# One more Strassen block in three of the four down-projection pairs of a hybrid decoder layer

## The chip, the cores and the metric

The kernel runs on one core of one Trainium2 chip. The metric is the device time in microseconds (us) of one execution, as the median of several runs. Engine names are those of the profile: PE is TensorE, DVE is VectorE, ACT is ScalarE, POOL is GpSimd, SP is SyncE; PEld is PE's loading of its stationary operand.

## What is computed

One layer of a hybrid decoder trunk on 256 tokens of width 2048: an RG-LRU branch and an attention branch, merged; a cross attention; and a SwiGLU feed-forward of inner width 5632, whose last product, the down projection, is what the change touches.

```python
def swiglu(h, w_gate, w_up, w_down):
    return (jax.nn.silu(h @ w_gate) * (h @ w_up)) @ w_down
...
    h = rmsnorm(x, norm_ffn_g[l])
    x = x + swiglu(h, w_ffn_gate[l], w_ffn_up[l], w_ffn_down[l])
return rmsnorm(x, norm_final_g)
```

## The kernel before

Every large product is done in split single precision. A weight tile `w_raw` (256 rows of the weight, as two tiles of 128, by 512 columns, 512 KB) is loaded by SP's queue. ACT rounds it to `w_hi` (L838), DVE takes the rest `w_lo` (L1228), and PE adds three matmuls for each product (L473 to L475): hi by hi, hi by lo, lo by hi. A **chunk** is one such weight tile in one of R = 4 slots. PE consumes chunks in order. ACT writes `w_hi` of chunk m when PE has finished chunk m-4, DVE follows with `w_lo`, and PE waits for that before chunk m. On ACT and DVE the function `splits` runs a stage's other work of chunk c first and then the weight step of chunk c+4, so everything on these engines stands in one fixed order.

Most stages are **pairs**: two groups of 512 output columns (two PSUM buffers, `group0` and `group1`) are made together over the same activations. A plan lists the steps, each for a k pair kp (256 values of k). `O5` makes two ordinary chunks, O5a for the first group and O5b for the second, of 12 matmuls each. `W4` makes a **Strassen block**: four chunks A, B, C, D of 6, 3, 6 and 6 matmuls, 21 in place of 24. A and B are loaded; C and D are sums of weight tiles, which DVE makes in `weight_sums` (L1243, L1244, L1246) just ahead of `w_lo` of A. A block also needs sums of activations, made once for each k pair (L1367 to L1370 on DVE, L870 on ACT, L1376 on DVE) and kept. `T6+7+8+9` makes four k pairs for the first group and then the same four for the second.

Four of the seven Strassen products of a block go to the extra PSUM tensors `side0` and `side1`. After the last D chunk of a pair, `fold_rest` and `first_fold` put them into the SBUF tile `fold` (ACT L876, DVE L1385, L1386, L1388, L1389) at chunks last_sum+1 and last_sum+2. At last_sum+3 and last_sum+4 DVE adds `fold` to the residual `x_res` (L1710, or L1734 in the last pair), once for each half of the tokens. At the last two chunks of a pair (counts -2 and -1) `add_group` (L1581) adds the two PSUM groups to `x_res`, and this hands the group's buffer to the next pair: PE may not start the next pair's first chunk of a group before it.

The feed-forward runs in two parts, a (six gate/up pairs, then two down pairs over 12 k pairs) and b (five gate/up pairs, then two down pairs over 10). The gate/up pair j makes four tiles of the inner activations, which are transposed and split during the next pair (`inner_split`, `inner_rest`); where `F_SUMS` names the k pair 2(j-1), its activation sums are made there too. Two steps of the final norm lie in the last down pair, ("b", 2): `squares` (ACT L885) at chunks 1 and 3, and `gained` (DVE L1719) at chunks 6 and 8. The last four chunks are made token half by token half, so that the first half's tail runs beside the second's products.

Of the kernel before, what the change touches and what calls it, by code (L numbers as in the profile page):

```python
# [56 lines left out]
for _j in range(1, KG):  # L57
# [8 lines left out]
RNN_PLANS = {0: "T0+1 O3 W2 O5 W4 O6 O7".split(), 2: "O0 O1 W2 O3 O5 W4 O6 O7".split()}  # L66
KEY_PLAN = "O0 O1 W3 O2 O4 W5 O6 O7".split()
FIRST_UP_PLAN = "O0 O1 O2 W3 O4 W5 O6 O7".split()
DOWN_PLAN = {("a", 0): "O0 O1 O3 W2 O5 O7 W4 O8 W6 O9 O10 O11".split(),
             ("a", 2): "O0 O1 W2 O3 O5 W4 O7 W6 O9 W8 O10 O11".split(),  # L70
             ("b", 0): "O0 O1 O3 O5 W2 O6 W4 O7 O8 O9".split(),
             ("b", 2): "O0 O1 W2 O3 W4 O5 T6+7+8+9".split()}
R_SUMS = [int(_step[1:]) for _step in RNN_PLANS[0] if _step[0] == "W"]
K_SUMS = [int(_step[1:]) for _step in KEY_PLAN if _step[0] == "W"]
X_SUMS = [int(_step[1:]) for _step in UP_PLAN if _step[0] == "W"]
F_SUMS = {_part: sorted({int(_step[1:]) for (_of, _j), _plan in DOWN_PLAN.items() if _of == _part for _step in _plan if _step[0] == "W"})
          for _part in ("a", "b")}
# [27 lines left out]
for _part, _groups in (("a", FA), ("b", FB)):  # L105
    for _j in range(_groups):
        PLACED.append((("gate_" + _part, _j), ("up_" + _part, _j), FIRST_UP_PLAN if (_part, _j) == ("a", 0) else UP_PLAN))
    for _j in range(0, KG, 2):
        PLACED.append((("down_" + _part, _j), ("down_" + _part, _j + 1), DOWN_PLAN[_part, _j]))
_n = _g = 0  # L110
# [1693 lines left out]
```

How the kernel before makes its waits and increments, by code:

```python
        def wait_product(engine, end):  # L303
            s, used = slot_of(end - 1)
            engine.wait_ge(w_used[s], START + used + 1)
# [1 line left out]
        def wait_taken(engine, g):  # L308
            p, before = buf_of(g)
            engine.wait_ge(taken[p], START + before + 1)
# [3 lines left out]
        @block.sync  # L315
# [1 line left out]
            def load(n, w, row, col):  # L317
                s, _ = raw_of(n)
                if LOAD_OF[n] >= R:
                    earlier, used = slot_of(LOADED[LOAD_OF[n] - R])
                    sync.wait_ge(w_ready[earlier], START + used + 1)
                sync.dma_start(raw[:, s], w[row:row + CK * P, col:col + GW].rearrange("(k p) n -> p k n", p=P)).then_inc(raw_full[s], 16)
# [20 lines left out]
                sync.dma_start(raw[:, 0, k], w_in[k * P:(k + 1) * P, IN_COLS["g_rnn"]:IN_COLS["g_rnn"] + GW]).then_inc(signal, 16)  # L344
            for n, (name, c) in enumerate(OPENING):
                if name == "g_rnn" and c > 0:
                    x_pair(c)
                if n > 0:
                    load(n, w_in, c * CK * P, IN_COLS[name])
            for j in range(KG):
                if j > 0:
                    in_group("g_rnn", j)
                if j >= 2:
                    sync.wait_ge(sem("lru_z"), j - 1)
                for a, gate in enumerate(("lru_w_a", "lru_w_i")):
                    sync.dma_start(lw[j % 2][:, a], dram[gate][j * NB:(j + 1) * NB, :, :].rearrange("n k m -> k n m"))\
                        .then_inc(sem(f"lw_full{j % 2}"), 16)
```

## Time and profile before

| | |
|---|---|
| median of 3 runs | 1751.98 us (1751.96 to 1752.61) |
| profiled execution, first to last instruction | 1750.0 us |
| PE busy | 1738.3 us (99%) |
| DVE busy | 1287.1 us (74%) |
| ACT busy | 974.8 us (56%) |
| mean DMA rate | 193 GB/s |

The profiled execution is known by its span alone; it lies 1.98 us below the median of the timed runs. Matmuls overlap, so PE reads as busy nearly always: what one costs is the distance from its start to the next one's start. Times in the trace's rows are microseconds from the start of the span.

### The profile page before, as it was taken

To read this page: it belongs to the slowest core of one execution; us is meant where nothing else is said; L and a number is where in the kernel's file an instruction comes from. 1 tells how busy PE (TensorE), PEld (TensorE's weight loads), DVE (VectorE), ACT (ScalarE), POOL (GpSimd) and SP (SyncE) were. 2 spreads that over 40 slices of the span, in tenths; PEclk is the share of its full clock that TensorE was granted. 3 is DMA by queue.
4 is the path that set the end of the run, shared out by engine and by line. 5 is a ranking of instruction groups with operands and counts; after the bars stand their busy time and mean duration, and the time that the engine had idled before them with its cause. 6 is when DMAs were issued, how large, how long until landed. Compare 5 with 4: busy or idle time off the path is not lost.

```text
span 1750.0 us, 20314 instructions
## 1 busy us (share of the span) xinstructions
PE 1738.3 (99%) x7923; PEld 1442.6 (82%) x7923; DVE 1287.1 (74%) x1404; ACT 974.8 (56%) x1211; POOL 28.8 (2%) x54
## 2 busy tenths in 40 slices
PE   9999999999999999999999999999999999999998
PEld 7888888888888888888888888888888888888886
DVE  7677687887575757555565579888888788888787
ACT  6767668554555555544455465555555545555554
POOL 1100000000000000000000000000000000000000
PEclk9999999999999999999999999999999999999999
DMA  8565665666565655556755455566666565666664
GB/s 292 172 204 166 196 201 162 204 203 204 157 212 166 216 168 189 174 187 206 250 186 187 140 174 185 191 197 196 194 204 213 183 206 192 193 193 195 216 201 158
DMA packets 176047, 338.22 MB, mean 193 GB/s; under 512 B 10704, under 2 KB 15312, under 8 KB 175696
## 3 DMA queue, kind: packets, MB, share of 16 engines
q1 hardware_dynamic: 173376, 327.98, 59.5%
q0 software_dynamic: 1296, 5.24, 0.9%
q10 hardware_dynamic: 1280, 3.71, 0.5%
q8 instruction: 62, 1.02, 0.2%
q14 instruction: 33, 0.27, 0.1%
HBM read 334.80 MB, written 2.10 MB: 193 GB/s over the span
## 4 chain that ended last, share of the span: by engine, by line
PE 97%; DVE 1%; ACT 0%; issue 0%; DMA 0%; ACTq 0%; POOLq 0%; POOL 0%; DVEq 0%
PE group L473 29%; PE group L475 29%; PE group L474 29%; PE side L473 2%; PE side L474 2%; PE side L475 2%; PE side L536 2%; DVE w_lo L1228 0%; PE side L670 0%; PE side L654 0%; DMA x_T_in<-in_x_T 0%; PE side L608 0%; PE side L607 0%; PE side L606 0%; DVE x_res L1581 0%
## 5 line engine op out<-in xcount | busy, mean ns | idle before, releaser
L838 ACT ACTIVATE w_hi<-w_raw 128x1024 fp32r<-128x1024 f32 x612 | 622.4, 1028 | 538.5 <-PE group L475 437.2
L1228 DVE TENSOR_TENSOR w_lo<-w_raw,w_hi 128x1024 fp32r<-128x1024 f32 x612 | 711.8, 1184 | 281.4 <-ACT w_hi L838 275.0
L473 PE MATMUL group<-w_hi,x_hi 128*128 128x512 f32 x1460 | 573.3, 393 | 0.8 <-DVE w_lo L1296 0.6
L475 PE MATMUL group<-w_hi,x_lo 128*128 128x512 f32 x1460 | 568.8, 390 | 0.0
L474 PE MATMUL group<-w_lo,x_hi 128*128 128x512 f32 x1460 | 568.2, 389 | 0.0
L473 PEld LDWEIGHTS group<-w_hi,x_hi 128*128 128x128 f32 x1460 | 274.1, 188 | 59.1 <-DVE w_lo L1228 1.9
L475 PEld LDWEIGHTS group<-w_hi,x_lo 128*128 128x128 f32 x1460 | 274.0, 188 | 57.6
L474 PEld LDWEIGHTS group<-w_lo,x_hi 128*128 128x128 f32 x1460 | 274.2, 188 | 55.6
L838 ACT ACTIVATE w_hi<-w_sums 128x1024 fp32r<-128x1024 f32 x86 | 91.3, 1061 | 150.2 <-PE group L475 104.6
L1228 DVE TENSOR_TENSOR w_lo<-w_sums,w_hi 128x1024 fp32r<-128x1024 f32 x86 | 104.8, 1222 | 52.5 <-ACT w_hi L838 52.3
L473 PE MATMUL group<-w_hi,v_hi 128*128 128x512 f32 x296 | 115.9, 392 | 0.0
L475 PE MATMUL group<-w_hi,v_lo 128*128 128x512 f32 x296 | 115.2, 389 | 0.0
L474 PE MATMUL group<-w_lo,v_hi 128*128 128x512 f32 x296 | 115.1, 389 | 0.0
L473 PE MATMUL group<-w_hi,inner_hi 128*128 128x512 f32 x286 | 111.6, 390 | 0.0
L475 PE MATMUL group<-w_hi,inner_lo 128*128 128x512 f32 x286 | 111.3, 389 | 0.0
L474 PE MATMUL group<-w_lo,inner_hi 128*128 128x512 f32 x286 | 111.3, 389 | 0.0
L1243 DVE TENSOR_TENSOR w_sums<-w_raw 128x1024 f32<-128x1024 f32 x43 | 52.5, 1221 | 43.6 <-issue 21.3
L475 PEld LDWEIGHTS group<-w_hi,v_lo 128*128 128x128 f32 x296 | 55.6, 188 | 11.6
L473 PEld LDWEIGHTS group<-w_hi,v_hi 128*128 128x128 f32 x296 | 55.6, 188 | 11.3
L474 PEld LDWEIGHTS group<-w_lo,v_hi 128*128 128x128 f32 x296 | 55.6, 188 | 11.3
L475 PEld LDWEIGHTS group<-w_hi,inner_lo 128*128 128x128 f32 x286 | 53.7, 188 | 11.3
L473 PEld LDWEIGHTS group<-w_hi,inner_hi 128*128 128x128 f32 x286 | 53.7, 188 | 11.3 <-DVE x_res L1581 0.3
(304 smaller groups left out, 1714.4 us busy)
## 6 DMA issues: line engine op xcount, KB each, us to landing
w_raw<-in_w_in SPq DMA_DIRECT2D x223, 512.0 KB, 4.2
w_raw<-in_w_ffn_gate SPq DMA_DIRECT2D x88, 512.0 KB, 3.9
w_raw<-in_w_ffn_up SPq DMA_DIRECT2D x88, 512.0 KB, 4.6
w_raw<-in_w_ffn_down SPq DMA_DIRECT2D x88, 512.0 KB, 4.8
w_raw<-in_w_rnn_proj SPq DMA_DIRECT2D x32, 512.0 KB, 4.8
w_raw<-in_w_attn_proj SPq DMA_DIRECT2D x32, 512.0 KB, 4.2
w_raw<-in_w_mix_out SPq DMA_DIRECT2D x32, 512.0 KB, 3.7
w_raw<-in_w_xkv SPq DMA_DIRECT2D x16, 512.0 KB, 3.8
```

Source lines behind the costliest of these rows:

```text
L473: nc.tensor.matmul(out, h, whi[:, s, k, :], start=start, stop=False)
L474: nc.tensor.matmul(out, h, wlo[:, s, k, :], start=False, stop=False)
L475: return nc.tensor.matmul(out, l, whi[:, s, k, :], start=False, stop=stop)
L536: last = nc.tensor.transpose(dst[:, k, tt * P:(tt + 1) * P], src[:, tt, k * P:(k + 1) * P], ident)
L838: nc.scalar.activation(whi[:, s, ks], src[:, ks], ACT.Copy).then_inc(hi_ready[s], 1)
L1228: V_.tensor_tensor(wlo[:, s, ks], src[:, ks], whi[:, s, ks].bitcast(F32), ALU.subtract).then_inc(w_ready[s], 1)
L1243: then(V_.tensor_tensor(w_sums[:, :, 0, :], tiles[:, a:a + 4:3, :], tiles[:, a + 2:a + 3, :].to_broadcast([P, 2, GW]), ALU.add))
```

## The change

Only the table of plans changes. In ("a", 0) four blocks (kp 2, 4, 6, 8) replace three (2, 4, 6); in ("b", 0) three (2, 4, 6) replace two (2, 4); in ("b", 2) three (2, 4, 6) replace two (2, 4). ("a", 2) stays.

```diff
-DOWN_PLAN = {("a", 0): "O0 O1 O3 W2 O5 O7 W4 O8 W6 O9 O10 O11".split(),
+DOWN_PLAN = {("a", 0): "O0 O1 O3 W2 O5 W4 O7 W6 O9 W8 O10 O11".split(),
              ("a", 2): "O0 O1 W2 O3 O5 W4 O7 W6 O9 W8 O10 O11".split(),
-             ("b", 0): "O0 O1 O3 O5 W2 O6 W4 O7 O8 O9".split(),
-             ("b", 2): "O0 O1 W2 O3 W4 O5 T6+7+8+9".split()}
+             ("b", 0): "O0 O1 O3 W2 O5 W4 O7 W6 O8 O9".split(),
+             ("b", 2): "O0 W2 O1 W4 O3 W6 T5+7+8+9".split()}
```

`F_SUMS` is worked out from this table. Part a keeps 2, 4, 6, 8. Part b goes from 2, 4 to 2, 4, 6, so the activation sums of kp 6 are made anew, in the gate/up pair ("gate_b", 4).

The block nearest to the end of a pair moves later, and with it the fold. DVE at the end of ("a", 0), a piece of the difference:

```order
 L1228 TENSOR_TENSOR w_lo<-w_raw,w_hi 128x1024
 L1710 TENSOR_TENSOR x_res<-x_res,fold 128x1024
+L1581 TENSOR_TENSOR x_res<-x_res,group 128x2x512
 L1228 TENSOR_TENSOR w_lo<-w_raw,w_hi 128x1024
 L1710 TENSOR_TENSOR x_res<-x_res,fold 128x1024
-L1228 TENSOR_TENSOR w_lo<-w_raw,w_hi 128x1024
-L1581 TENSOR_TENSOR x_res<-x_res,group 128x2x512
-L1228 TENSOR_TENSOR w_lo<-w_raw,w_hi 128x1024
 L1581 TENSOR_TENSOR x_res<-x_res,group 128x2x512
 L1228 TENSOR_TENSOR w_lo<-w_raw,w_hi 128x1024
```

The two additions of the fold (L1710) and the two additions of the groups (L1581) stood in four different chunks and stand in two now.

DVE at the end of ("b", 0) and the start of ("b", 2), before:

```order
929 L1710 TENSOR_TENSOR x_res<-x_res,fold 128x1024
930 L1228 TENSOR_TENSOR w_lo<-w_raw,w_hi 128x1024
931 L1710 TENSOR_TENSOR x_res<-x_res,fold 128x1024
932 L1228 TENSOR_TENSOR w_lo<-w_raw,w_hi 128x1024
933 L1581 TENSOR_TENSOR x_res<-x_res,group 128x2x512
934 L1228 TENSOR_TENSOR w_lo<-w_raw,w_hi 128x1024
935 L1581 TENSOR_TENSOR x_res<-x_res,group 128x2x512
936 L1228 TENSOR_TENSOR w_lo<-w_raw,w_hi 128x1024
937 L1243 TENSOR_TENSOR w_sums<-w_raw 128x2x512
```

and in the changed kernel:

```order
946 L1710 TENSOR_TENSOR x_res<-x_res,fold 128x1024
947 L1581 TENSOR_TENSOR x_res<-x_res,group 128x2x512
948 L1243 TENSOR_TENSOR w_sums<-w_raw 128x2x512
949 L1244 TENSOR_TENSOR w_sums<-w_sums,w_raw 128x512
950 L1246 TENSOR_TENSOR w_sums<-w_sums,w_raw 128x512
951 L1228 TENSOR_TENSOR w_lo<-w_raw,w_hi 128x1024
952 L1710 TENSOR_TENSOR x_res<-x_res,fold 128x1024
953 L1581 TENSOR_TENSOR x_res<-x_res,group 128x2x512
954 L1228 TENSOR_TENSOR w_lo<-w_raw,w_hi 128x512
```

The next pair's first block has moved from its chunk 4 to its chunk 2, so its weight sums (L1243, L1244, L1246) have come to stand between the two L1581, where they stood behind both.

DVE in the middle of ("b", 2), around the two `gained` steps (L1719), before:

```order
944 L1719 TENSOR_TENSOR x_res<-x_res,gain_final 128x2x512
945 L1243 TENSOR_TENSOR w_sums<-w_raw 128x2x512
946 L1244 TENSOR_TENSOR w_sums<-w_sums,w_raw 128x512
947 L1246 TENSOR_TENSOR w_sums<-w_sums,w_raw 128x512
948 L1228 TENSOR_TENSOR w_lo<-w_raw,w_hi 128x1024
949 L1228 TENSOR_TENSOR w_lo<-w_raw,w_hi 128x512
950 L1719 TENSOR_TENSOR x_res<-x_res,gain_final 128x2x512
951 L1228 TENSOR_TENSOR w_lo<-w_sums,w_hi 128x1024 x2
```

and in the changed kernel:

```order
957 L1243 TENSOR_TENSOR w_sums<-w_raw 128x2x512
958 L1244 TENSOR_TENSOR w_sums<-w_sums,w_raw 128x512
959 L1246 TENSOR_TENSOR w_sums<-w_sums,w_raw 128x512
960 L1228 TENSOR_TENSOR w_lo<-w_raw,w_hi 128x1024
961 L1228 TENSOR_TENSOR w_lo<-w_raw,w_hi 128x512
962 L1719 TENSOR_TENSOR x_res<-x_res,gain_final 128x2x512
963 L1228 TENSOR_TENSOR w_lo<-w_sums,w_hi 128x1024 x2
964 L1719 TENSOR_TENSOR x_res<-x_res,gain_final 128x2x512
```

The two `gained` steps stood on both sides of the second block's weight sums; now they stand on both sides of its `w_lo` of C and D. SP's queue issues the same 217 rows in the same order in both kernels.

## Rows read from the trace of the kernel before

**Rows 1.** The page: the span, and each engine's busy time.

```profile
span 1750.0 us, 20314 instructions
...
PE 1738.3 (99%) x7923; PEld 1442.6 (82%) x7923; DVE 1287.1 (74%) x1404; ACT 974.8 (56%) x1211; POOL 28.8 (2%) x54
```

**Rows 2.** PE's waits from 20 us on: total us, times, longest us.

```profile
PE side L473 <- DVE w_lo L1228: 0.5, 1, 0.5
PE group L473 <- DVE x_res L1581: 0.2, 1, 0.2
```

**Rows 3.** Timeline, PE, the last products: start, duration, engine, line, out<-in.

```profile
1735.61 0.39 PE L473 MATMUL group<-w_hi,inner_hi 128*128 128x512 f32 x1
...
1742.19 0.39 PE L475 MATMUL group<-w_hi,inner_lo 128*128 128x512 f32 x1
```

**Rows 4.** Timeline, DVE, from the end of ("a", 2) into ("gate_b", 0).

```profile
1417.19 1.22 DVE L1581 TENSOR_TENSOR x_res<-x_res,group 128x1024 f32<-128x1024 f32 x1
1418.33 1.22 DVE L1228 TENSOR_TENSOR w_lo<-w_raw,w_hi 128x1024 fp32r<-128x1024 f32 x1
1419.46 1.22 DVE L1710 TENSOR_TENSOR x_res<-x_res,fold 128x1024 f32<-128x1024 f32 x1
1420.71 1.22 DVE L1581 TENSOR_TENSOR x_res<-x_res,group 128x1024 f32<-128x1024 f32 x1
...
1422.99 1.22 DVE L1243 TENSOR_TENSOR w_sums<-w_raw 128x1024 f32<-128x1024 f32 x1
...
1425.68 1.82 DVE L1228 TENSOR_TENSOR w_lo<-w_raw,w_hi 128x1024 fp32r<-128x1024 f32 x2
```

**Rows 5.** Timeline, PE, the same place; in brackets idle time and its releaser.

```profile
1421.37 0.39 PE L475 MATMUL group<-w_hi,x_lo 128*128 128x512 f32 x1
1421.99 0.50 PE L473 MATMUL group<-w_hi,x_hi 128*128 128x512 f32 x1 [0.23 <-DVE x_res L1581]
1422.33 0.40 PE L474 MATMUL group<-w_lo,x_hi 128*128 128x512 f32 x1
```

**Rows 6.** Timeline, ("gate_b", 3): activation sums on DVE, and PE just behind.

```profile
1562.32 0.28 DVE L1367 TENSOR_TENSOR inner_sums<-inner_T_in 128x128 f32<-128x128 f32 x1
```

```profile
1564.35 0.39 PE L475 MATMUL side<-w_hi,x_sums_lo 128*128 128x512 f32 x1
1564.64 0.50 PE L473 MATMUL group<-w_hi,x_hi 128*128 128x512 f32 x1
```

**Rows 7.** Timeline, ("b", 2): DVE, then PE, then ACT.

```profile
1709.91 1.22 DVE L1719 TENSOR_TENSOR x_res<-x_res,gain_final 128x1024 f32<-128x1024 f32 x1
1711.05 2.35 DVE L1228 TENSOR_TENSOR w_lo<-w_sums,w_hi 128x1024 fp32r<-128x1024 f32 x2
1713.32 4.63 DVE L1228 TENSOR_TENSOR w_lo<-w_raw,w_hi 128x1024 fp32r<-128x1024 f32 x4
...
1712.32 0.50 PE L473 MATMUL side<-w_hi,inner_sums_hi 128*128 128x512 f32 x1 [0.54 <-DVE w_lo L1228]
...
1697.85 0.62 ACT L885 ACTIVATE junk<-x_res 128x512 f32<-128x512 f32 x1
...
1699.61 1.06 ACT L838 ACTIVATE w_hi<-w_sums 128x1024 fp32r<-128x1024 f32 x1 [0.43 <-PE group L475]
```

**Rows 8.** Stretches behind the last matmul: us, busy of PE, ..., PEclk, DMA.

```profile
1742.60:1747.20 4.60, 0.00 (x0) 0.00 (x0) 2.21 (x6) 2.06 (x5) 0.55 (x1) 1.00 0.69 260
1747.40:1750.00 2.60, 0.00 (x0) 0.00 (x0) 0.00 (x0) 0.00 (x0) 0.00 (x0) 0.50 0.59 232
```

**Rows 9.** Weight tiles: an issue, the median time to landing, ACT's longest wait here.

```profile
1410.61 0.37 SPq L323 DMA_DIRECT2D w_raw<-in_w_ffn_up  x1
...
w_raw<-in_w_ffn_down SPq DMA_DIRECT2D x88, 512.0 KB, 4.8
...
1680.06 1.06 ACT L838 ACTIVATE w_hi<-w_raw 128x1024 fp32r<-128x1024 f32 x1 [3.90 <-DMA w_raw<-in_w_ffn_down]
```

**Rows 10.** Timeline, DVE, the second token half of the output's tail.

```profile
1742.61 0.75 DVE L1748 TENSOR_TENSOR x_res<-x_res,group 128x256 f32<-128x256 f32 x2 [0.81 <-PE group L475]
```

## The prediction, made before the changed kernel ran

> **What bounds the kernel now.** I read the page first, then PE's waits, then the timeline of DVE, ACT and PE at the seams between the down pairs. PE is busy for 99% of the span [rows 1] and behind the opening waits for anyone only twice, 0.7 us in all [rows 2], so every matmul that goes away is time won and every gap in PE is time lost. The last products show what a matmul costs: 30 rows stand from 1735.61 to 1742.19 [rows 3], that is 6.58 / 29 = 0.227 us from start to start. An ordinary chunk (12 matmuls) takes 2.72 us, a Strassen block (21) 4.76 us where two ordinary chunks take 5.44.
>
> The two waits are 0.23 us where ("gate_b", 0) waits for a buffer [rows 5] and 0.54 us in ("b", 2) [rows 7]. But DVE is close behind. A block costs it the weight sums (2.69 us from 1422.99 to 1425.68 [rows 4]) and `w_lo` of four chunks, 1.13 + 0.69 + 1.13 + 1.23 = about 4.2 us, so 6.9 us against 4.76 on PE; the two ordinary chunks around it must pay that back (2.3 against 5.44). One block and one ordinary pair together are 9.2 on DVE and 10.2 on PE: about 1.0 us to spare, and each other step of DVE there is 1.22.
>
> **What the change gives.** Three blocks more, each 3 matmuls less: 9 x 0.227 = **-2.04 us**, all on the path. Inside ("a", 0) and ("b", 0) it costs nothing: the rhythm O W O W is the one that ("a", 2), which the change leaves alone, runs now, and neither of PE's two waits [rows 2] lies in it. ACT (56% busy [rows 1]) has room, and SP issues the same loads.
>
> **The seam ("a", 0) to ("a", 2).** The end of ("a", 0) becomes what the end of ("a", 2) is now: L1710, L1581, `w_lo`, L1710, L1581. There the second L1581 runs from 1420.71 to 1421.93 [rows 4], and PE, which would have started its next matmul at 1421.37 + 0.23 = 1421.60, starts at 1421.99, with 0.11 us more to the following one [rows 5] and about 0.06 over the next few: 0.39 + 0.17 = **+0.56 us**. Now this seam has nothing of it; the cover that goes is the distance of two chunks between fold and group additions. Bounds: 0 (were DVE 0.4 us earlier) and 0.8; I take the copy.
>
> **The activation sums of kp 6 in ("gate_b", 4).** The words of the change hold for part a, not for part b. The four small DVE steps from 1562.32 on push back one `w_lo`, and PE starts at 1564.64 where 1564.35 + 0.23 = 1564.58 was due [rows 6]; with the slower restart (0.11 and a little) this is **+0.20 us**. Bounds 0.1 to 0.3. The rest of it (ACT's copies, L1376) stands where DVE has over 2 us in hand.
>
> **The seam ("b", 0) to ("b", 2), the largest term.** Before, the weight sums of the next pair's first block stand behind both L1581. Now they stand between them, with `w_lo` of A. Up to the first L1581 the order is again that of ("a", 2): it ends at 1418.41 on the clock of [rows 4]. Then come, instead of one `w_lo` (1418.33 to 1419.46), the sums (2.69) and `w_lo` (1.13): L1710 starts 2.69 us later than 1419.46, the second L1581 ends 2.69 later than 1421.93, at 1424.62, and PE restarts 0.06 later, at 1424.68, against 1421.60 due. The stall is 3.08 us and the restart 0.17: **+3.26 us**. The queue behind the second L1581 is `w_lo` of B, C and D, but these are released by PE's own late chunks: B has 0.69 us of work against the 2.72 us that PE then needs for O0b. The sums need the tiles A and B: the copy of B's load is issued at 1410.61 and takes 4.8 us as a median [rows 9], so it is there by 1415.4, and 1418.33 is when it is wanted. From below, the first L1581 can't start before PE has ended its chunk, two chunks before the due start: 1421.60 - 5.44 = 1416.16, with a matmul's length about 1416.4. In the copy it starts 0.8 us later than that, so a DVE that comes early would make the term 2.5; from above, 0.4 us of lateness in front of it makes 3.7. The copy is the nearest row, for fold and group additions have the same distance to the last block. What goes in return is a delay of 0.1 us that L1581 causes now at this seam: **-0.11 us** (PE's first chunk of ("b", 2) takes 2.83 us instead of 2.72).
>
> **Inside ("b", 2).** Now PE waits once, before chunk C of the second block: idle 0.54, plus 0.16 by which a matmul's 0.39 us is longer than the pitch, plus the restart's 0.17, is 0.87; with traces of slowness before and behind I take 0.90 us [rows 7]. Its cause is DVE's load of sums, two L1719 and `w_lo` between the first D and this C. In the changed kernel the first L1719 takes exactly the place of the second, just before `w_lo` of C, and the earlier place is free: 1.14 us won. But `squares` at chunk 3 now stands ahead of `w_hi` of O1b. It lasts from 1697.85 to 1699.18 (1699.61 less the 0.43 idle [rows 7]), and makes this `w_hi` and its `w_lo` 1.07 us late. C therefore waits 0.78 instead of 0.85. Then the second L1719 stands between `w_lo` of D and of O3a. Before, the next ordinary `w_lo` ran from 1713.32 to 1714.54 [rows 7], 0.67 us before PE wanted it (1712.32 + 0.17 + 12 x 0.227 = 1715.21). It will be 1.14 - 0.07 later and PE 0.07 earlier, so it is 0.47 us too late; with 0.05 for the signal and 0.17 for the restart 0.69. After that DVE has its 1.0 us a round again and W6 costs nothing. Sum 0.78 + 0.69 + 0.05 = 1.52 against 0.90: **+0.62 us**. Bounds: -0.1 (only the first of the two waits) and +1.4 (each wait one `w_lo` share later).
>
> **The tail.** The four last chunks, the last L1581 and the last L1719 keep their order against PE; DVE ends by waiting 0.81 us for PE's last product [rows 10], so up to 0.8 us of delay there is covered: 0.
>
> **Sum.** -2.04 + 0.56 + 0.20 + 3.26 - 0.11 + 0.62 = **+2.49 us**. On the profiled execution's span this is 1750.0 + 2.5 = 1752.5; the timed median lies 1.98 above the span, so 1751.98 + 2.5 = **1754.5 us**, 0.14% slower. A measurement of this kernel tells about 0.2% (3.5 us) from no change, so this counts as within it. With the bounds of the terms partly offsetting one another, this case's own range is 1753.4 to 1755.4.
>
> **Rivals.**
> A. *DVE comes early to all three places.* It then starts the first L1581 with the end of PE's chunk (0.8 us less at the last seam), costs nothing at the first seam (0.56 less) and meets O3a in time (0.69 less): 1754.5 - 2.05 = 1752.4. For it: the spare microsecond of each round. Against it: `w_hi` is released by PE, four chunks back, so DVE can't run ahead of PE by more than that, and its place at the end of a pair is that of the copy. Chance 0.12.
> B. *The clock falls in the long stall*, the case that ends slower. PE would stand idle for 2.9 us at the start of O0b of ("b", 2), longer than anywhere in the rows of before. With PE idle from 1742.6 on, the granted clock stayed 1.00 for 4.6 us and was 0.50, that is 1.2 instead of 2.4 GHz, from 1747.4 on [rows 8]. If it fell in the 2.9 us gap, the products behind it run at half rate; for as long as the 4.6 us of those rows this costs 2.3 us: 1754.5 + 2.3 = 1756.8. It decides (slower by over 0.2%) once the low clock lasts for 2 us of products. Against it: the row held its clock for longer than 2.9 us. Chance 0.07. The Trainium skill (TensorE: Matmul & The Clock Gate, Why this matters for your kernels) advises against idle gaps between bursts of matmuls, since an idle stretch brings back the half rate; by that rule this rival would be the forecast, and the trace neither confirms nor excludes it for a gap of this length.
> C. *Weight tiles or DVE later than in the copies.* The sums between the two L1581 need the tile B 7.7 us after its issue (1418.33 - 1410.61 [rows 9]). ACT once waited 3.90 us for a tile [rows 9] at just this seam; such a delay on top of 4.8 is 1.0 us too late and goes one to one into the stall; in the denser rounds of ("b", 0), where `gain_final` is loaded too, another 1.0 to 1.5 can come. 1755.5 to 1757. Chance 0.13.
>
> **How the numbers follow.** Forecast 0.62, A 0.12, B 0.07, C 0.13, the rest (terms that I don't see) 0.06, of which 0.02 faster, 0.02 same, 0.02 slower. Within 0.2%: 0.62 + 0.12 + 0.02 = 0.76. Slower: 0.07 + 0.13 + 0.02 = 0.22. Faster: 0.02, since the whole gain of 2.04 us is less than 3.5. For 8 in 10 the range takes in the forecast, the upper part of A and most of C: 1752.6 to 1756.6.
>
> **What would show it.** In the profile after: nine matmuls less; a PE gap of about 2.9 us released by L1581 one chunk into ("b", 2), and 0.23 us at the start of ("a", 2)'s second chunk; two PE gaps released by `w_lo` in the second block of ("b", 2), before C and before O3a; a new set of L1367 to L1370 in ("gate_b", 4); PEclk 1.00 throughout. Wrong would be: a gap below 2.3 us at the last seam (A), a clock below 1.00 behind it (B), or gaps released by a DMA or by `w_lo` inside ("b", 0) (C).

## The result and the profile after

The changed kernel is slower: 1757.42 us as the median of 9 runs (1755.42 to 1759.13), beside 1752.05 us for the kernel before measured with it (9 runs, 1750.92 to 1753.74). The ratio is 1.003, with a 95% interval from 1.0022 to 1.0039. The prediction had 1754.5 us with a range up to 1756.6, so the sign of its sum was right, but the loss was more than twice as large as forecast, and it fell out of "within 0.2%" and out of the range.

The page of the changed kernel, its span and busy times, against [rows 1]:

```profile
span 1754.9 us, 20339 instructions
PE 1738.7 (99%) x7914; PEld 1441.8 (82%) x7914; DVE 1300.7 (74%) x1424; ACT 980.4 (56%) x1219; POOL 28.8 (2%) x54
```

PE has nine matmuls less and still a longer span, by 4.9 us. Its waits from 20 us on (who waited <- for whom: us in total, times, longest), against [rows 2]:

```profile
PE group L473 <- DVE x_res L1581: 4.2, 4, 3.0
PE side L473 <- DVE w_lo L1228: 0.4, 1, 0.4
PE group L473 <- DVE w_lo L1228: 0.3, 1, 0.3
```

Two waits have become six. The largest is the one that the prediction named, at the second chunk of ("b", 2). DVE there (start, duration, engine, line), against the end of ("a", 2) in [rows 4]:

```profile
1686.88 1.22 DVE L1581 TENSOR_TENSOR x_res<-x_res,group 128x1024 f32<-128x1024 f32 x1
1688.02 1.22 DVE L1243 TENSOR_TENSOR w_sums<-w_raw 128x1024 f32<-128x1024 f32 x1
1689.28 0.69 DVE L1244 TENSOR_TENSOR w_sums<-w_sums,w_raw 128x512 f32<-128x512 f32 x1
1690.12 0.69 DVE L1246 TENSOR_TENSOR w_sums<-w_sums,w_raw 128x512 f32<-128x512 f32 x1
1690.72 1.22 DVE L1228 TENSOR_TENSOR w_lo<-w_raw,w_hi 128x1024 fp32r<-128x1024 f32 x1
1691.86 1.22 DVE L1710 TENSOR_TENSOR x_res<-x_res,fold 128x1024 f32<-128x1024 f32 x1
1693.11 1.22 DVE L1581 TENSOR_TENSOR x_res<-x_res,group 128x1024 f32<-128x1024 f32 x1
```

and PE in the same place:

```profile
1691.01 0.39 PE L475 MATMUL group<-w_hi,inner_lo 128*128 128x512 f32 x1
1694.39 0.50 PE L473 MATMUL group<-w_hi,inner_hi 128*128 128x512 f32 x1 [3.00 <-DVE x_res L1581]
1694.73 0.40 PE L474 MATMUL group<-w_lo,inner_hi 128*128 128x512 f32 x1
...
1695.46 0.63 PE L474 MATMUL group<-w_lo,inner_hi 128*128 128x512 f32 x1
1695.89 0.63 PE L475 MATMUL group<-w_hi,inner_lo 128*128 128x512 f32 x1
...
1698.02 0.63 PE L474 MATMUL group<-w_lo,inner_hi 128*128 128x512 f32 x1
1698.45 0.56 PE L475 MATMUL group<-w_hi,inner_lo 128*128 128x512 f32 x1
1698.85 0.40 PE L473 MATMUL side<-w_hi,inner_hi 128*128 128x512 f32 x1
```

The second L1581 stands exactly where the copy put it, with the weight sums ahead of it, and PE is idle for 3.00 us. Then something comes that the forecast did not have: from 1695.46 on eight matmuls stand about 0.43 us apart instead of 0.227 and last 0.56 to 0.63 instead of 0.39 us. The stretches (us, PE busy with its count, PEclk, DMA share, GB/s) say why:

```profile
1690.00:1694.00 4.00, 1.39 (x7) 1.00 0.17 50
1694.00:1698.00 4.00, 3.61 (x10) 0.67 0.64 207
1698.00:1702.00 4.00, 4.00 (x17) 0.90 0.01 5
1702.00:1706.00 4.00, 4.00 (x19) 1.00 0.44 130
```

The granted clock is below 1.00 in both middle stretches, although PE is at work there. This is rival B. In this execution it came not while PE stood idle but about a microsecond after it had started again, and it lasted for 1698.85 - 1695.46 = 3.4 us. The Trainium skill (TensorE: Matmul & The Clock Gate, Why this matters for your kernels) warns of such idle gaps; the trace of after agrees with it, at a gap of 3.00 us.

The seam into ("a", 2) is the second place of interest, against [rows 5]:

```profile
1355.21 0.39 PE L475 MATMUL group<-w_hi,inner_lo 128*128 128x512 f32 x1
1355.87 0.50 PE L473 MATMUL group<-w_hi,inner_hi 128*128 128x512 f32 x1 [0.27 <-DVE x_res L1581]
...
1358.50 0.39 PE L475 MATMUL group<-w_hi,inner_lo 128*128 128x512 f32 x1
1359.40 0.50 PE L473 MATMUL group<-w_hi,inner_hi 128*128 128x512 f32 x1 [0.51 <-DVE x_res L1581]
```

PE waits there twice, not once. The loss of a chunk is the time from the start of the last matmul of the chunk ahead to the start of its own last matmul, less 2.72 us (1.36 and 0.68 for the chunks of a block). The losses give this account of the profiled executions:

| place | forecast, us | profile after less before, us |
|---|---|---|
| nine matmuls | -2.04 | -2.04 |
| seam into ("a", 2): O0a, O0b | +0.56 | +1.38 (0.57 + 0.81) |
| seam into ("gate_b", 0) | 0 | +0.20 (0.76, before 0.56) |
| ("gate_b", 4), activation sums | +0.20 | +0.19 |
| seam into ("b", 2): O0a, O0b, and the step into A2 | +3.26 - 0.11 | +4.90 - 0.11 (O0b 4.72, A2 0.18) |
| inside ("b", 2): C4, O3a | +0.62 | +0.55 (0.75 + 0.65, before 0.85) |
| opening | 0 | -0.2 |
| sum | +2.49 | +4.9 |

Of the 4.90 us at the last seam, 8 x (0.427 - 0.227) = 1.6 us is the low clock, and 3.3 us is what was forecast as 3.26. What has to be explained are the 1.6 us of clock and the 0.8 + 0.2 us at the two other seams.

### The profile page after: what moved, and what is told of

It is laid out like the page before. It is cut to its first block, busy times and chain, and to the rows that moved or that the text cites. A ratio compares the mean times of both kernels' runs of the same rounds, so it can differ in the third digit from the quotient of the medians.

```text
span 1754.9 us, 20339 instructions
## 1 busy us (share of the span) xinstructions
PE 1738.7 (99%) x7914; PEld 1441.8 (82%) x7914; DVE 1300.7 (74%) x1424; ACT 980.4 (56%) x1219; POOL 28.8 (2%) x54
## 4 chain that ended last, share of the span: by engine, by line
PE 92%; DVE 4%; DMA 2%; ACT 1%; issue 1%; ACTq 0%; POOLq 0%; POOL 0%; DVEq 0%
PE group L473 27%; PE group L475 27%; PE group L474 27%; DMA w_raw<-in_w_ffn_down 2%; PE side L536 2%; PE side L473 2%; PE side L474 2%; PE side L475 2%; DVE w_lo L1228 1%; ACT w_hi L838 1%; DVE x_res L1581 0%; DVE x_res L1710 0%; PE side L670 0%; PE side L654 0%; DVE w_sums L1243 0%
## 5 line engine op out<-in xcount | busy, mean ns | idle before, releaser
L838 ACT ACTIVATE w_hi<-w_sums 128x1024 fp32r<-128x1024 f32 x92 | 97.6, 1061 | 163.3 <-PE group L475 110.2
L1228 DVE TENSOR_TENSOR w_lo<-w_sums,w_hi 128x1024 fp32r<-128x1024 f32 x92 | 112.1, 1222 | 54.1 <-ACT w_hi L838 53.9
L473 PE MATMUL group<-w_hi,inner_hi 128*128 128x512 f32 x268 | 105.5, 394 | 4.1 <-DVE x_res L1581 3.8
L474 PE MATMUL group<-w_lo,inner_hi 128*128 128x512 f32 x268 | 105.0, 392 | 0.0
L475 PE MATMUL group<-w_hi,inner_lo 128*128 128x512 f32 x268 | 105.0, 392 | 0.0
L1243 DVE TENSOR_TENSOR w_sums<-w_raw 128x1024 f32<-128x1024 f32 x46 | 56.1, 1220 | 39.0 <-issue 20.9
```

The lines of the kernel that those rows point to most:

```text
L473: nc.tensor.matmul(out, h, whi[:, s, k, :], start=start, stop=False)
L474: nc.tensor.matmul(out, h, wlo[:, s, k, :], start=False, stop=False)
L475: return nc.tensor.matmul(out, l, whi[:, s, k, :], start=False, stop=stop)
L838: nc.scalar.activation(whi[:, s, ks], src[:, ks], ACT.Copy).then_inc(hi_ready[s], 1)
L1228: V_.tensor_tensor(wlo[:, s, ks], src[:, ks], whi[:, s, ks].bitcast(F32), ALU.subtract).then_inc(w_ready[s], 1)
L1243: then(V_.tensor_tensor(w_sums[:, :, 0, :], tiles[:, a:a + 4:3, :], tiles[:, a + 2:a + 3, :].to_broadcast([P, 2, GW]), ALU.add))
```

## The experiments

Each kernel is named by its label. "After" is the changed kernel, and a loss is that of a chunk as in the table; losses are read from one profiled execution of each kernel. The kernels were run in four sets, each beside the kernel before, whose medians were 1752.23 us (`fill12`, `fill6`, `sums_behind`, `b2_back`), 1751.81 (`after_again`, `fill12_again`, `tiles_gate`, `all_three`), 1752.21 (`code_moved`, `only_a0`, `only_b2`) and 1751.83 (`longer_stall`).

### Is VectorE's order at the last seam the main price?

`b2_back`: the changed kernel with the old plan of ("b", 2).

```
-             ("b", 2): "O0 W2 O1 W4 O3 W6 T5+7+8+9".split()}
+             ("b", 2): "O0 O1 W2 O3 W4 O5 T6+7+8+9".split()}
```

> The changed kernel with the plan of ("b", 2) as before; ("a", 0) and ("b", 0) keep their added block. Theory: the 3.3 us of the last seam, about 2.1 us of clock and 0.6 inside ("b", 2) go, the 0.68 us of one block comes back, and the seam ("b", 0) to ("b", 2) costs a copy of the 0.56: 1757.4 - 3.3 - 2.1 - 0.6 + 0.7 + 0.6 = 1752.7. Rival (each added block loses about as much as the others): a third goes, 1755.6.

`sums_behind`: the plans of the changed kernel, but at the end of ("b", 0) DVE's weight step of the second-to-last chunk (weight sums and `w_lo` of A) comes behind the second L1581.

```
 for c in range(count):
     yield c
+    if behind and c == count - 2:
+        continue
+    for m in ((n + c + LEAD - 1, n + c + LEAD) if behind and c == count - 1 else (n + c + LEAD,)):
```

> The changed kernel with one thing undone: on DVE, at the end of ("b", 0), the weight step of chunk count-2 (with the weight sums of the next pair's first block) stands behind the second L1581 instead of between the two. Theory: the 3 us wait goes but for 0.3 us before chunk A, and the clock stays up: 1757.4 - 2.9 - 2.1 = 1752.4. Rival (the wait comes from late weight tiles or from DVE's general load): at most 1 us is won, 1756.4 or more.

Measured: `b2_back` 1752.98 us (10 runs, ratio to before 1.0006, 0.9997 to 1.0016), `sums_behind` 1753.72 us (10 runs, 1.001, 1.0000 to 1.0019). Neither shows a stall of 3 us or a low clock at this seam. In `b2_back` O0a loses 0.10 us and O0b 0.82, with the short wait that its expectation puts there as a copy of the 0.56:

```profile
1692.92 0.50 PE L473 MATMUL group<-w_hi,inner_hi 128*128 128x512 f32 x1 [0.53 <-DVE x_res L1581]
```

Further in, the old wait at C4 is left (0.82). In `sums_behind` O0b loses nothing; left are 0.69 at A2, whose `w_lo` now comes late, 0.82 at C4 and 0.68 at O3a. `b2_back` came within 0.3 us of its expected 1752.7; `sums_behind` was expected at 1752.4 and came out 1.3 us above that, still far below its rival's 1756.4. So putting four DVE instructions a place further back, with the same blocks, matmuls and bytes, wins 3.7 us of the 5.4. The order is the cause of the largest term, not the number of blocks.

`only_b2`: the kernel before with the new plan of ("b", 2) alone.

```
-             ("b", 2): "O0 O1 W2 O3 W4 O5 T6+7+8+9".split()}
+             ("b", 2): "O0 W2 O1 W4 O3 W6 T5+7+8+9".split()}
```

> The kernel before with the new plan for ("b", 2) alone, which starts with O0 W2: the weight sums come between the two L1581, while ("b", 0) ends as before with two ordinary pairs between its last block and the seam, so that its folds are early. Theory that VectorE's queue between the two L1581 is the price, 2.69 + 1.13 us of it: the first L1581 starts with the end of TensorE's chunk, two chunks ahead, and the stall is 2.3 us less a matmul's length, about 2.3 to 2.5 us instead of 3.0, so the chunk O0b loses 2.5 to 2.7 us, 4 or more if the clock falls with it; with 0.6 us inside and 0.68 won about 2.5 to 4 us over the kernel before. Rival, that the stall needs the late folds of the new ("b", 0) too: under 1 us at O0b, and the time within 0.5 us of the kernel before.

Measured: 1753.50 us (10 runs, 1.0007, 0.9998 to 1.0017), loss of O0b 1.14 us. The theory missed this (2.5 to 2.7 at O0b, the time 2.5 to 4 us over the kernel before, measured 1.3), and so did its rival (under 1). DVE in `only_b2`:

```profile
1680.42 1.22 DVE L1710 TENSOR_TENSOR x_res<-x_res,fold 128x1024 f32<-128x1024 f32 x1
1681.67 1.23 DVE L1228 TENSOR_TENSOR w_lo<-w_raw,w_hi 128x1024 fp32r<-128x1024 f32 x1
1682.81 1.22 DVE L1710 TENSOR_TENSOR x_res<-x_res,fold 128x1024 f32<-128x1024 f32 x1
1684.07 1.22 DVE L1228 TENSOR_TENSOR w_lo<-w_raw,w_hi 128x1024 fp32r<-128x1024 f32 x1
1685.48 1.22 DVE L1581 TENSOR_TENSOR x_res<-x_res,group 128x1024 f32<-128x1024 f32 x1 [0.20 <-PE group L475]
...
1690.46 1.22 DVE L1581 TENSOR_TENSOR x_res<-x_res,group 128x1024 f32<-128x1024 f32 x1
```

With the old ("b", 0) both L1710 stand ahead of the first L1581, and that one waits for PE (0.20 us) instead of being late. Its second L1581 starts 4.98 us behind the first; in the changed kernel it is 1693.11 - 1686.88 = 6.23, since an L1710 stands between them too. From the start of the first L1581 to the end of the second it takes 4.98 + 1.22 = 6.20 us there, and the first starts 5.25 us ahead of the time at which O0b is due (1690.50 + 0.23 - 1685.48): that leaves 0.95 us of delay, and O0b lost 1.14 with the slower restart. The expectation's 2.69 and 1.13 us with the two L1581 added would have given this. So the stall of 3.0 us needs both plans. In the profiles O0b loses 0.82 us with the new ("b", 0) alone (`b2_back`), 1.14 with the new ("b", 2) alone, and 3.3 without the clock's share with both, more than the two together. Against `only_b2` the L1710 in between adds 1.25 us, and the first L1581 starts 0.9 us later against PE.

### Is the low clock a price of the stall?

`fill12`, `fill6`: the changed kernel with 12 or 6 matmuls whose result is unused in PE's program, ahead of the wait for the second L1581 at the last seam.

```
+                if c == 1:
+                    pe.wait_ge(sem("folded"), folds)
+                    filled, turn = slot_of(N0[first] + 1)
+                    pe.wait_ge(w_ready[filled], START + turn + 1)
+                    for _ in range(12):
+                        nc.tensor.matmul(P7, inner_hi[:, 0, tok0], whi[:, filled, 0, :], start=True, stop=True)
```

> The changed kernel with 12 more matmuls of 512 columns on PE ahead of O0b of ("b", 2), just where PE stands idle for 3.0 us; their product is overwritten and used by nobody, everything else is as in the changed kernel. Theory (the clock): the gap lets the granted clock fall, and that costs the part of the loss that the forecast lacks; 12 x 0.227 = 2.7 us of filling leaves a gap of 0.3 us at the same end of the wait, so the clock stays at 1.00 and the time falls from 1757.4 to about 1755.3, with less spread between the runs. Rival (the wait alone, or late tiles): the end of the wait doesn't move, so the time stays at 1757.4.

> As the run with 12 more matmuls, but with 6 (1.36 us), which leaves PE idle for about 1.6 us. Theory (the clock): the shorter idle time makes the fall rarer or absent, 1755.3 to 1756.4; were the idle time's length without effect, 1757.4. Rival (the wait alone): 1757.4.

`after_again` and `fill12_again` are the changed kernel and `fill12` once more, side by side.

> The changed kernel once more, so that the others of this call stand beside it on one chip. All theories: about 5 us over the kernel before, near 1757.4. If the slow clock behind the stall at ("b", 2) belongs to the stall, the profile shows it again: matmuls 0.43 us apart instead of 0.227 for some 3 us from about 1 us after the restart. If it was an accident of the one profiled execution, the matmuls behind the stall stand 0.227 us apart.

> The changed kernel with 12 matmuls of unused results (TensorE busy for about 2.7 us) in the stall ahead of the second chunk of ("b", 2). They end about when VectorE's x_res is ready, so they cost nothing or a few tenths. Theory that the clock falls because TensorE is idle, in most executions: 1.6 us less than after_again, about 1755.8, at most 3.5 us of extra time in that chunk. Rival, that the fall is rare or costs the median nothing: the same as after_again within 0.5 us.

`fill12` in the profile, PE's timeline:

```profile
1691.04 2.88 PE L809 MATMUL side<-w_hi,inner_hi 128*128 128x512 f32 x12
1694.40 0.50 PE L473 MATMUL group<-w_hi,inner_hi 128*128 128x512 f32 x1 [0.49 <-DVE x_res L1587]
1694.74 0.40 PE L474 MATMUL group<-w_lo,inner_hi 128*128 128x512 f32 x1
```

and its stretches:

```profile
1690.00:1694.00 4.00, 3.92 (x18) 1.00 0.18 53
1694.00:1698.00 4.00, 3.60 (x16) 1.00 0.64 208
```

DVE releases the buffer as late as before, but PE is at work meanwhile: the clock stays 1.00, and O0b with the step into A2 loses 3.50 us (3.46 in `fill12_again`) where the changed kernel loses 4.90 and, in `after_again`, 5.10. `fill6` left 1.81 us idle and lost 3.46, with full clock too. The medians side by side: `after_again` 1758.31 us (5 runs), `fill12_again` 1756.41 us (8 runs), 1.9 us less where 1.6 was expected. The first set, taken alone, spoke for the rival: `fill12` came out at 1757.08 (10 runs) where the theory had 1755.3 and the rival 1757.4, and `fill6` at 1757.49 (8 runs) where the theory had at most 1756.4.

The mean granted clock of each execution separates them better, if it is read with care. PE is idle at the end of every execution, and the clock falls there too, so the mean also holds how long that last low stretch was: 2.2 to 5.6 us in the profiles. `fill6` and `fill12_again` read 0.998 in their profiled executions without any fall at the seam; all five profiles with one read 0.998 as well. With a fall at the seam a mean of 0.999 would need a last stretch under 1.9 us, shorter than in any profile, so 0.999 is taken for no fall; 0.998 can be either. Of 14 executions of the changed kernel, 4 show 0.999 (median 1755.6 us) and 10 show 0.997 or 0.998 (1758.2 us). Of 18 executions with 12 fillers, 16 show 0.999, like the kernel before with 73 of 81. With 6 fillers it is 3 of 8, which suggests that half a filling often doesn't help; its one profile has no fall, so this isn't shown.

`longer_stall`: `only_b2` with the first weight-sum operation of that block carried out twice more.

```
+                for _ in range(2 if m == N0["down_b", 2] + 2 else 0):
+                    then(V_.tensor_tensor(w_sums[:, :, 0, :], tiles[:, a:a + 4:3, :], tiles[:, a + 2:a + 3, :].to_broadcast([P, 2, GW]), ALU.add))
```

> The run with the new plan for ("b", 2) alone, and in it the first weight-sum operation of that pair's first block carried out twice more (same operands, same result, 1.26 us each with the wait for its own end), between the two L1581. VectorE has 2.52 us more there and nothing else changes, so TensorE's idle time ahead of O0b grows from 0.85 to about 3.4 us. Theory that the length of the idle time brings the clock down: the matmuls behind it stand 0.427 us apart for about 3 us, as in the profiles of the changed kernel, the chunk O0b loses 1.14 + 2.52 + 1.5 = about 5.2 us, and the median is some 3.5 to 4 us over that of the new plan alone, about 1757.3. Rival, that the fall has to do with something else that the changed kernel does there: O0b loses 3.7 us, the matmuls stand 0.227 us apart, and the median is 1756.0.

Measured: 1757.50 us (8 runs, 1.003, 1.0020 to 1.0041), 4.0 us over `only_b2`, as the theory had it, and O0b loses 5.07 us. PE's timeline, and the stretch behind the stall:

```profile
1691.42 0.39 PE L475 MATMUL group<-w_hi,inner_lo 128*128 128x512 f32 x1
1695.17 0.80 PE L473 MATMUL group<-w_hi,inner_hi 128*128 128x512 f32 x1 [3.36 <-DVE x_res L1583]
1695.77 0.63 PE L474 MATMUL group<-w_lo,inner_hi 128*128 128x512 f32 x1
```

```profile
1694.00:1698.00 4.00, 2.83 (x7) 0.61 0.60 176
```

2.52 us more of DVE's time cost 3.9 us in O0b, the surplus again at 0.427 us a matmul, in a kernel with the old plans everywhere else. The stall's length brings the clock down; the changed kernel's other edits are not needed for it.

### Why does the seam into ("a", 2) cost 1.4 us?

`only_a0`: the kernel before with the new plan of ("a", 0) alone.

```
-DOWN_PLAN = {("a", 0): "O0 O1 O3 W2 O5 O7 W4 O8 W6 O9 O10 O11".split(),
+DOWN_PLAN = {("a", 0): "O0 O1 O3 W2 O5 W4 O7 W6 O9 W8 O10 O11".split(),
```

> The kernel before with the new plan for ("a", 0) alone, one block more. Three matmuls less are 0.68 us won. If the seam into ("a", 2) costs what the prediction put, 0.56: 0.1 us less than before. If it costs what the profile after showed, 1.4, with the late first tile: 0.7 us more than before, about 1752.8; nothing else changes in the profile.

Measured: 1753.47 us (10 runs, 1.0007, 0.9998 to 1.0017), 1.3 us over the kernel before where 0.7 was expected; in the profile 0.32 and 0.78 us lost at O0a and O0b, and 0.74 instead of 0.56 at the seam into ("gate_b", 0), which had not been expected. Most of the excess comes with this plan alone. ACT in the changed kernel shows what DVE was late for:

```profile
1348.47 1.06 ACT L838 ACTIVATE w_hi<-w_raw 128x1024 fp32r<-128x1024 f32 x1 [2.11 <-DMA w_raw<-in_w_ffn_down]
```

At the place that was copied ACT waited for PE, 1.18 us, and not for a load. The tile of O0a was issued with the same lead, 11.67 us ahead of the time at which its chunk was due (1355.44 - 1343.77, and 1418.88 - 1407.21 at the copied place), but landed after 4.7 us instead of 3.7.

`tiles_gate`: the first six chunks of ("a", 2) and ("b", 2) loaded from w_ffn_gate, whose tiles land after 3.9 us as a median on the page of before, against 4.8 for w_ffn_down [rows 9].

```
-                    if half is not None:
+                    if half is not None and c < 6 and first in (("down_a", 2), ("down_b", 2)):
+                        load(N0[first] + c, dram["w_ffn_gate"], kp * CK * P, cols[half])
+                    elif half is not None:
```

> The changed kernel with the first six chunks of ("a", 2) and of ("b", 2) loaded from w_ffn_gate instead of w_ffn_down (so its output isn't the reference's). The waits, steps and bytes are the same. Theory that the seam ("a", 0) to ("a", 2) costs 1.38 instead of 0.56 us because tiles of w_ffn_down land later: the first two chunks of ("a", 2) lose 0.5 to 0.7 us together, ScalarE no longer waits over 1 us for a tile there, and the time is 0.8 us less than after_again, about 1756.6. Rival, that VectorE is late of itself: the seam keeps 1.3 to 1.5 us and the time stays.

Measured: 1757.07 us (5 runs), losses 0.52 and 0.79 at this seam, 1.3 together. The median is 1.2 us below `after_again`, but the ranges of the two overlap (1756.7 to 1759.1 and 1756.5 to 1759.6), and the seam kept its loss. The first tile takes 4.6 us from w_ffn_gate too (the three behind it land sooner, 4.8 to 5.1 us instead of 5.6 to 7.1, which leaves the loss as it was). The source theory falls; the rival "VectorE is late of itself" doesn't fit either, since ACT still waited 2.02 us for the load.

The next theory came from the profile's queues. The changed kernel, first the load of O0a alone (issue: count, KB each, us to landing), then the queues from 1343 to 1349 (packets, MB, share of the 16 engines):

```profile
w_raw<-in_w_ffn_down SPq DMA_DIRECT2D x1, 512.0 KB, 4.7
```

```profile
q1 hardware_dynamic: 618, 1.18, 66.5%
q8 instruction: 1, 0.02, 1.4%
```

A packet of an instruction queue, 16 KB, starts 1.1 us behind this issue; at the copied place, 1407 to 1413 in the kernel before, there is none, and the tile takes 3.7 us:

```profile
q1 hardware_dynamic: 807, 1.56, 77.5%
```

```profile
w_raw<-in_w_ffn_gate SPq DMA_DIRECT2D x1, 512.0 KB, 3.7
```

Such packets come every 28 us or so (62 of them on the page). All ten profiles with this plan of ("a", 0) and unmoved packets have one that starts 1.0 to 2.6 us behind this issue, and the tile takes 4.4 to 6.3 us in them. `code_moved` moves the packets: 160 waits more that are already met, early in PE's program.

```
+MORE = [("g_rnn", 1), ("xr", 1), ("g_rnn", 2), ("xr", 2), ("g_rnn", 3)]
...
                             done = products(gps[p][:, tt, :], xh[:, kt, tok], xl[:, kt, tok], s, k, kt == 0, kt == tiles - 1)
+                            for _ in range(2 if (stage, j) in MORE else 0):
+                                pe.wait_ge(w_ready[s], START + used + 1)
```

> The changed kernel with 160 waits more in TensorE's program, all of them met already, one after every third matmul of the input products early in the program (about 600 us before the seams). What is computed, loaded and waited for stays. Theory: the profile's instruction queue q8 carries TensorE's own program, a packet of 16 KB every 28 us (about 123 matmuls, with their weight loads some 250 instructions), and the one that starts 1.1 us behind the first load of ("a", 2) is why that tile takes 4.5 to 6.3 us instead of 3.7. 160 instructions more put each packet some 17.5 us earlier, clear of all three seams: the first tile of ("a", 2) then takes 3.7 to 3.9 us, the first two chunks lose 0.5 to 0.7 instead of 1.38 us together, and apart from what the waits themselves cost the time is 0.7 us less, about 1756.8. Rival, that the tile is late for another reason (its rows, or the order of the loads): 4.5 us or more and 1.3 to 1.5 us as before, though the packet has moved.

Measured: the same load, the queues from 1344 to 1350 (this kernel is 1.0 us later here), and the timeline of ACT and PE (a line of the code is up to three higher here, so L1584 is L1581):

```profile
w_raw<-in_w_ffn_down SPq DMA_DIRECT2D x1, 512.0 KB, 3.9
```

```profile
q1 hardware_dynamic: 669, 1.28, 78.3%
```

```profile
1348.70 1.06 ACT L841 ACTIVATE w_hi<-w_raw 128x1024 fp32r<-128x1024 f32 x1 [1.31 <-DMA w_raw<-in_w_ffn_down]
...
1359.63 0.50 PE L474 MATMUL group<-w_hi,inner_hi 128*128 128x512 f32 x1 [0.29 <-DVE x_res L1584]
```

The packet has gone, from 1344.9 to 1328.0, so q8 does carry PE's program. The tile takes 3.9 us, O0a loses nothing, and O0b loses 0.58 us where the prediction had put 0.56. At the seam into ("gate_b", 0) the loss is back to 0.53. The median, 1757.24 us (8 runs), is 0.5 us below the 1757.8 of the changed kernel's 14 runs, less than such medians can tell; the verdict rests on one profile of `code_moved` against the ten others. Over all fourteen profiles, take the weight tiles that were issued at most 0.5 us before all tiles ahead had landed, with the next issue within 1.3 us. Behind 47 of them a packet of q8 started within 2.6 us, and these took 4.2 to 5.6 us (median 4.8); of the 833 others the median is 3.85, and 46 took over 4.2 us.

### A version without the three late starts

`all_three`: the changed kernel with the second-to-last weight step behind the second L1581 in the three down pairs that another pair follows, and the two `gained` steps of ("b", 2) at chunks 8 and 16 instead of 6 and 8. (The expectation names the edit otherwise, with all four down pairs and with activation sums of ("gate_b", 0); the code cut shows what was run.)

```
-                    for c in splits(N0[first], count):
+                    for c in splits(N0[first], count, True):
...
-                if c == 6:
+                if c == 8:
                     gained(0)
-                if c == 8:
+                if c == 16:
                     gained(1)
```

> The changed kernel with the second-to-last chunk's weight step put behind the second L1581 at the end of all four down pairs, and the two activation-sum pieces in ("gate_b", 0) moved to chunks 8 and 16. Theory that the loss is VectorE's order at the seams: the seam of ("b", 2) loses under 0.5 instead of 4.9 us, the seams into ("a", 2) and ("gate_b", 0) under 0.3 each instead of 1.4 and 0.8, so 1757.4 - 4.4 - 1.1 - 0.5 = about 1751.4, and down to 1750 if the clock is also full; faster than the kernel before by 0.5 to 2 us. Rival, that the three blocks more overload VectorE wherever the steps stand: the waits move on to the next w_lo and the time stays above 1753.

Measured: 1750.99 us (11 runs, 0.9996, 0.9987 to 1.0005), beside 1751.81 us for the kernel before. The seams are nearly free: nothing at O0b of ("a", 2) and ("gate_b", 0), where 0.8 us each were lost, with 0.52 us left at O0a of ("a", 2) for the late tile. But in ("b", 2) 0.50 us at O0a, 0.96 at A2 and 0.37 at O3a remain, so part of the load moved on to the next `w_lo`, as the rival said; its time, above 1753, did not come. The wait at C4 is gone with the `gained` step that stood ahead of it. The median is 7.3 us below the change as made (`after_again`, 1758.31) and not told apart from the kernel before.

## Why the prediction was wrong

**What bounds the kernel, and the gain**: right. Nine matmuls were 2.04 us, and no chunk inside ("a", 0) or ("b", 0) lost anything by the denser rhythm O W O W.

**The seam into ("a", 2)**: the mechanism was right and its size too, for VectorE: 0.58 us in `code_moved` against 0.56. What failed is the step "I take the copy": the copied place had no instruction packet among its tiles and this place has. That adds 0.8 us here, which brings the term to 1.38, above its upper bound of 0.8. The seam into ("gate_b", 0) lost 0.2 us more than before, and `code_moved` took away that too (0.53); a packet of q8 begins at 1406.0 there, 1.7 us ahead of the first load, so for this one the link is the run's, not a row's. The other profiles bear it out: where the packet starts 1.1 to 1.8 us ahead of that load (seven profiles) PE's wait at this seam is 0.27 to 0.51 us, and where it starts over 2.1 us ahead (six) the wait is 0.23 us, as before the change.

**Activation sums in ("gate_b", 4)**: +0.19 against +0.20.

**The seam into ("b", 2)**: the order, the length of the stall (3.00 us idle against 2.9) and the restart were right; without the clock the term is 3.3 against 3.26. That the first L1581 starts on the copy's clock held as well, 4.36 us ahead of the time at which O0b is due against 4.41 in the copy. The step that failed, and the largest miss, is the one that left the clock out of the sum. Rival B had the mechanism, and its price was close: 2.3 us for 4.6 us at half rate, measured 1.6 us for 3.4. The argument that gave it only 0.07 was that in [rows 8] the granted clock stays 1.00 for 4.6 us after the last matmul. Two things were wrong with it. First, that row ends with PE idle and nothing to run. In the changed kernel's profile the clock was 1.00 all through the idle time as well, and fell after the restart: the row showed how long the record stays high, not how long a gap may be without a price. Second, the 4.6 us were one execution's. All fourteen profiles end in the same way, and the clock falls from 2.1 us (`fill6`) to 5.3 us (`tiles_gate`) after PE's last product has ended:

```profile
1748.20:1750.30 2.10, 0.00 (x0) 1.00 1.06 395
1750.40:1755.60 5.20, 0.00 (x0) 0.50 0.58 218
```

In the five stalls it fell 3.1 to 4.1 us after the last product ahead of them. A row in which PE starts again behind a gap would have been the one to look for, and the trace of before has none of more than 0.54 us past the opening. With no such row, the rule against idle gaps that the prediction cites for rival B from the Trainium skill (TensorE: Matmul & The Clock Gate, Why this matters for your kernels) deserved the larger chance.

**Inside ("b", 2)**: +0.55 against +0.62; both waits came where they were put (idle 0.44 us before C and 0.35 before O3a):

```profile
1711.74 0.50 PE L473 MATMUL side<-w_hi,inner_sums_hi 128*128 128x512 f32 x1 [0.44 <-DVE w_lo L1228]
1715.15 0.50 PE L473 MATMUL group<-w_hi,inner_hi 128*128 128x512 f32 x1 [0.35 <-DVE w_lo L1228]
```

**Rivals A and C**: in the changed kernel DVE came early at none of the three places. C, a tile later than in the copy, did happen, at the first seam rather than the last in the profiled execution; in `after_again` also at the last one, where O0b's tile took 7.1 us and O0a lost 1.55. B and C happened together, and the range, whose upper end stood at either of them alone, could not hold their sum: 1754.5 + 1.6 + 0.8 + 0.2 = 1757.1, against 1757.42 measured. That the two lie so close is partly luck: the terms are those of one execution, and the runs spread over 3.7 us.

What stays open: the 12 fillers leave the changed kernel's median 4.6 to 4.9 us above the kernel before, more than the profile's terms without the clock (4.9 - 1.6 = 3.3), and its executions at full mean clock still range from 1755.4 to 1759.0 us. The late tiles at the seams differ from one execution to the next and may be that spread: with the same instructions there, O0a of ("a", 2) loses from 0.32 us (`only_a0`) to 2.16 us (`fill6`, whose tile took 6.3 us), and why that tile was so late is open. The spread wasn't measured apart.

## What to carry over

- A stall's cost on a saturated TensorE is its length plus what the clock takes behind it. Price a planned gap of some 3 us with the surcharge (here 1.6 us, in most executions), and if it can't be removed, put work whose result nobody needs into it (here 12 matmuls, 1.9 us less).
- How long the clock stayed up in one idle stretch of one execution says little: the same stretch gave 2.1 to 5.3 us in fourteen profiles.
- When a term is copied from another place of the trace, compare everything that runs there: the loads' landing times and the instruction-queue packets too, not only the order of the engines' instructions.
- At a handover of buffers ask which long steps stand between the two releases. Moving four VectorE instructions behind the second release gave back 3.7 us, more than the three Strassen blocks were worth (2.04).

## What the runs showed of the hardware

- With 3.0 to 3.4 us of TensorE idle time the granted clock fell between 0.3 us before the restart and 1.0 us behind it, in all five profiles with such a stall (after, `after_again`, `tiles_gate`, `code_moved`, `longer_stall`), and stayed at 0.50 for 3.4 us in each, with products 0.427 us apart. With 0.4 to 1.8 us idle behind filler matmuls, 0.85 us in `only_b2`, or 1.25 us ahead of O0a in `after_again`, the profiles showed 0.227 us.
- The fetch of TensorE's own program shares the DMA engines with the weight tiles: a 16 KB packet about every 28 us, behind which a 512 KB tile took 4.8 instead of 3.85 us as a median if the packet started within 2.6 us behind that tile's issue. The packets move when instructions are added hundreds of microseconds earlier: 160 waits that were already met moved one by 17 us.
